# A hybrid streaming encoder on one core: modulation vectors of the reading in and of the first output projection computed on TensorE

## What is computed

```python
cond = silu(c)
for layer in range(4):
    mod = cond @ ada_w[layer] + ada_b[layer]        # 1024 -> 3 * 1024
    shift, scale, gate = split(mod, 3)
    h = rms_norm(x, norm_w[layer]) * (1.0 + scale) + shift
    y = mixer[layer](h)     # RG-LRU, gated DeltaNet, pooling, windowed attention; each ends with @ w_out
    x = x + gate * y
return rms_norm(x, final_norm_w)
```

## Time and profile before

| | |
|---|---|
| median of 3 runs | 3574.63 us (3570.79 to 3578.21) |
| the profiled execution | 3582.37 us |
| its span | 3580.6 us |
| mean granted TensorE clock | 0.968 |
| PE / DVE / ACT / POOL busy, share of the span | 93% / 64% / 42% / 26% |
| instructions | 49279 |

### The profile page before, as it was taken

One profiled execution on the slowest core, in us unless ns is written; L12 is line 12 of the kernel. 1 busy time (PEld: TensorE's weight loads), 2 busy tenths in 40 slices (PEclk: granted clock), 3 DMA queues, 4 the chain that ended last, 5 costly groups with the idle time before them and its releaser, 6 DMA issues.

```text
span 3580.6 us, 49279 instructions
## 1 busy us (share of the span) xinstructions
PE 3331.5 (93%) x18911; PEld 2689.9 (75%) x18911; DVE 2303.9 (64%) x3820; ACT 1509.9 (42%) x2635; POOL 943.0 (26%) x487
## 2 busy tenths in 40 slices
PE   5998899799999999999989999988998999999998
PEld 3776678677887777888767777876778777788877
DVE  6887888763466774565557766996536554556554
ACT  4665365333344124322466655653334431342234
POOL 1003233211233124222510043432121422422233
PEclk9999899899999999999989999998999999999999
DMA  4434455434753532111231123554449221221112
GB/s 170 131 111 129 126 145 147 124 105 127 251 179 89 166 93 88 50 37 36 65 129 55 46 72 84 159 139 111 126 112 349 74 59 53 60 72 40 32 48 100
DMA packets 569015, 383.83 MB, mean 107 GB/s; under 512 B 67802, under 2 KB 522445, under 8 KB 568781
## 3 DMA queue, kind: packets, MB, share of 16 engines
q1 hardware_dynamic: 568781, 380.68, 35.6%
HBM read 299.01 MB, written 80.54 MB: 106 GB/s over the span
## 4 chain that ended last, share of the span: by engine, by line
PE 71%; DVE 16%; DMA 4%; ACT 4%; issue 4%; SPq 1%; POOL 1%; ACTq 0%; DVEq 0%; POOLq 0%
PE bank L230 55%; DVE dnp_conv L1837 3%; DVE dnp_diag_term L1915 2%; DVE h_lo L700 1%; PE bank L2359 1%; DVE res_ada_sums L279 1%; DVE dnp_diag_inv L1918 1%; PE bank L2562 1%; DVE res_h L688 1%; DMA dn_planes<-dnp_inv_t 1%; PE bank L2589 1%; POOL w_lo L212 1%; PE bank L1527 1%; DVE res_sq_total L727 1%; PE bank L2603 1%
## 5 line engine op out<-in xcount | busy, mean ns | idle before, releaser
L230 PE MATMUL bank<-h_hi,w_hi 128*128 128x512 f32 x3616 | 1478.9, 409 | 49.6 <-DVE h_lo L126 16.0
L230 PE MATMUL bank<-h_hi,w_lo 128*128 128x512 f32 x3616 | 1428.0, 395 | 0.0
L230 PE MATMUL bank<-h_lo,w_hi 128*128 128x512 f32 x3616 | 1427.6, 395 | 0.0
L212 POOL TENSOR_TENSOR w_lo<-w_raw,w_hi 128x1024 fp32r<-128x1024 f32 x262 | 648.2, 2475 | 1447.8 <-ACT w_hi L203 1447.8
L230 PEld LDWEIGHTS bank<-h_hi,w_hi 128*128 128x128 f32 x3616 | 691.1, 191 | 227.4 <-issue 57.1
L230 PEld LDWEIGHTS bank<-h_lo,w_hi 128*128 128x128 f32 x3616 | 692.0, 191 | 148.6 <-issue 12.8
L230 PEld LDWEIGHTS bank<-h_hi,w_lo 128*128 128x128 f32 x3616 | 689.7, 191 | 150.8
L1837 DVE SCALAR_TENSOR_TENSOR dnp_conv<-dnp_raw,dn_conv_w,dnp_conv 128x512 f32<-128x512 f32 x288 | 267.1, 928 | 238.4 <-ACT dnp_conv L1659 231.1
L203 ACT ACTIVATE w_hi<-w_raw 128x1024 fp32r<-128x1024 f32 x292 | 306.1, 1048 | 71.5 <-DMA w_raw<-in_pool_w_in 24.8
L757 DVE SCALAR_TENSOR_TENSOR x_res<-bank,mod_gate,x_res 128x512 f32<-128x512 f32 x128 | 95.8, 749 | 268.6 <-PE bank L230 267.8
L844 ACT ACTIVATE res_sq<-x_res 128x512 f32<-128x512 f32 x160 | 101.0, 631 | 327.4 <-DVE x_res L757 225.4
(11 more groups left out here) (321 smaller groups left out, 4485.5 us busy)
## 6 DMA issues: line engine op xcount, KB each, us to landing
dnr_in<-dn_planes SPq DMA_DIRECT2D x112, 512.0 KB, 7.3
dn_planes<-y SPq DMA_DIRECT2D x192, 256.0 KB, 2.5
w_raw<-in_dn_w_in SPq DMA_DIRECT2D x64, 512.0 KB, 4.5
w_raw<-in_swa_w_in SPq DMA_DIRECT2D x36, 512.0 KB, 3.6
w_raw<-in_rg_w_in SPq DMA_DIRECT2D x32, 512.0 KB, 4.8
w_raw<-in_rg_w_out SPq DMA_DIRECT2D x32, 512.0 KB, 3.9
w_raw<-in_dn_w_out SPq DMA_DIRECT2D x32, 512.0 KB, 3.9
w_raw<-in_pool_w_in SPq DMA_DIRECT2D x32, 512.0 KB, 4.4
```

The source lines that it names most:

```text
L212: alu.tensor_tensor(self.lo[j % SLOTS][:, :, :], self.raw[j % 2][:, :, :], self.hi[j % SLOTS][:, :, :].bitcast(F32), ALU.subtract).then_in ...
L230: ins = self.nc.tensor.matmul(out, w[slot][:, k, :], x[:, k, cols], start=(k == 0 and n == 0), stop=(k == KT - 1 and n == 2))
```

## The change

Modulation gets a second way to its result, `multiply`. PE takes each piece as the stationary operand, 128 columns at a time, with column k of cond as the moving operand, and accumulates over k in PSUM bank 3. No running sums are kept (accs is 0), and `accumulate` and `reduce` aren't called in these two phases. PE's products release the pieces' buffers (`used`), and `finish` waits for the last of them. In the reading in PE does piece j after the transposes of step j; in the phase after layer 0 it does four pieces at the end of each of steps 3 to 14. The other two uses of the class stay as they are.

```diff
--- before.py
+++ after.py
@@ -250,6 +250,7 @@
         self.piece = places or [core.sb(f"{tag}_ada{i}", [P, cols], F32, ctx)[:, :] for i in range(bufs)]
         self.bufs = len(self.piece)
         self.acc = [core.sb(f"{tag}_ada_sums{i}", [P, cols], F32, ctx) for i in range(accs)]
+        self.products = 0
         self.loaded = [core.sem(f"{tag}_ada_loaded{i}") for i in range(self.bufs)]
         self.used = core.sem(f"{tag}_ada_used")
         self.summed = core.sem(f"{tag}_ada_summed")
@@ -288,8 +289,24 @@
                                         self.core.ones[:, 0:1], start=True, stop=True)
         ins.then_inc(self.summed, 1)
 
+    def multiply(self, pe, first, last):
+
+        n = self.cols // P
+        for m in range(first, min(last, self.pieces)):
+            t, k = divmod(m, KT)
+            pe.wait_ge(self.loaded[m % self.bufs], 16 * (m // self.bufs) + 16)
+            for i in range(n):
+                ins = self.nc.tensor.matmul(self.bank[:, t * n + i:t * n + i + 1],
+                                            self.piece[m % self.bufs][:, i * P:i * P + P], self.core.cond[:, k:k + 1],
+                                            start=(m == 0 and i == 0), stop=(m == self.pieces - 1 and i == n - 1))
+            ins.then_inc(self.used, 1)
+            self.products = m + 1
+
     def finish(self, dve):
-        dve.wait_ge(self.summed, len(self.blocks))
+        if self.products:
+            dve.wait_ge(self.used, self.pieces)
+        else:
+            dve.wait_ge(self.summed, len(self.blocks))
         core, V = self.core, self.nc.vector
         st = Steps(dve, self.ready)
         for i, (layer, part) in enumerate(self.jobs):
@@ -561,9 +578,9 @@
         ada, late = None, None
         if half == 0 and ingest:
             places = [core.before_h[:, i, :] for i in range(2 * KT)]
-            ada = Modulation(core, ctx, A, [(0, SHIFT), (0, SCALE)], tag, core.bank[3], D, 0, 2, places)
+            ada = Modulation(core, ctx, A, [(0, SHIFT), (0, SCALE)], tag, core.bank[3], D, 0, 0, places)
         elif half == 0 and layer == 0 and depth > 2:
-            late = Modulation(core, ctx, A, [(1, GATE), (2, SHIFT), (2, SCALE)], tag, core.bank[3], CH, 6, 2)
+            late = Modulation(core, ctx, A, [(1, GATE), (2, SHIFT), (2, SCALE)], tag, core.bank[3], CH, 6, 0)
         cs = [slice(c * CH, c * CH + CH) for c in range(NCH)]
         steps = [(c, d) for c in range(NCH) for d in range(KT)]
         split_ab = layer == 0 and depth > 1
@@ -660,8 +677,10 @@
                     sum_squares(c - 1)
                 if final and j > TURN_LAG - 1:
                     turn_x(j - TURN_LAG)
-                if late and j >= 6 and j % 2 == 0:
-                    late.reduce(pe, (j - 6) // 2)
+                if ada:
+                    ada.multiply(pe, j, j + 1)
+                if late and 3 <= j <= 14:
+                    late.multiply(pe, 4 * (j - 3), 4 * (j - 2))
             if final:
                 for j in range(len(steps) - TURN_LAG, len(steps)):
                     turn_x(j)
@@ -669,11 +688,6 @@
                 sum_squares(NCH - 1)
             else:
                 core.sum_last = lambda: sum_squares(NCH - 1)
-            if late:
-                late.reduce(pe, 5)
-            if ada:
-                for t in range(len(ada.blocks)):
-                    ada.reduce(pe, t)
             pe.wait_ge(s_x, len(steps) - 1)
             core.leave(pe, "pe")
 
@@ -768,12 +782,7 @@
                     continue
                 if c > 0 and not ada:
                     norm_dve(dve, c - 1, d)
-                if ada and c > 0:
-                    ada.accumulate(dve, d, d + 1)
-                if late and 3 <= j <= 14:
-                    late.accumulate(dve, 4 * (j - 3), 4 * (j - 2))
             if ada:
-                ada.accumulate(dve, KT, ada.pieces)
                 ada.finish(dve)
                 for k in range(KT):
                     norm_dve(dve, 0, k)
```

## The result

The change makes the kernel slower: 3648.2 us in the median of four runs (3635.4 to 3653.5), against 3574.6 before, a ratio of 1.0192 with a 95% interval of 1.0175 to 1.0209. A second series of the same kernel gave 3649.6 us and 1.0205 (1.0189 to 1.0221). The forecast was 3643, in a range of 3608 to 3668.

A forecast was written before the change was run, and what follows sets the result against it. VectorE was taken to end both stretches before the change; +34 us in the reading in and +34 in the projection on a profiled 3582.4 us gave 3650, less 7.7 us to the runs' median, 3643; range 3608 to 3668.

The forecast's parts named there:

- What bounds the stretches: Reading in and first projection of half 0: VectorE ends last before the change, though TensorE is busy 93% of the span.
- Price of a pair: One weight load and matmul on TensorE: 0.1125 us in a dense stream, 0.22 us in the reading in.
- Reading in: Start of the kernel: 256 pairs on TensorE's path make it +34 us, bounds +5 and +39.
- Piece 0: Reading in: TensorE's first group waits for the first piece, taken to land at 21.0 us.
- POOL's cover: End of the reading in: POOL's subtractions now run beside VectorE's chain instead of beside an accumulation, +2 us.
- The lower bound of +5: Least cost allowed for the reading in, with all pairs at the dense price.
- Projection: First output projection of half 0: 31.3 us removed, 43.2 added, and 22 of clock, sum +34 us, bounds +12 and +89.
- Clock: Projection: ten of twelve thin groups let TensorE's clock fall, 2.2 us lost each, +22 us, bounds 0 and +77.
- (a): Rival: the clock holds through the projection's groups, between dense matmuls; +46 us, 3621; chance 0.17.
- (b): Rival: the pairs keep the clock up everywhere, also in the reading in; +17 us, 3592; chance 0.07.
- (c): Rival, faster: weight loads slip beneath neighbouring work on TensorE in both stretches, 0.06 us a pair, 3558; chance 0.03.
- (d): Rival: clock falls are longer, or TensorE waits for pieces it now releases itself; up to 3698; chance 0.05.

The follow-up runs named there:

- e_reading: Changed kernel with the projection's accumulations put back on VectorE, so only the reading in is changed; 3609.0 us, ratio 1.0096 to the kernel before.
- e_proj: Changed kernel with the reading in's accumulations put back on VectorE, so only the projection is changed; 3625.5 us, ratio 1.0132 to the kernel before.
- e_spread: Changed kernel with each projection step's four pieces split, one behind each 6 dense matmuls instead of four behind 24; 3629.8 us, ratio 1.0143 to the kernel before.
- e_two: Changed kernel with each projection step's pieces put two behind 12 dense matmuls and two behind 24; one run, 3627.4 us.
- e_warm: Changed kernel with three added idle-work matmuls (six before the first piece) ahead of each piece's group in the reading in; one run, 3647.1 us.
- same_before: The kernel before, unchanged, run again for a second profile and its spread; 3575.9 us, ratio 1.0003.
- h_late: Kernel before with the projection's pieces shared, two of each four accumulated on VectorE and two multiplied on TensorE; 3578.9 us, ratio 0.9996 to the kernel before.
- h_both: As h_late, and TensorE also takes four of the reading in's 16 pieces, VectorE the other twelve; 3577.8 us, ratio 0.9996 to the kernel before.
- e_three: Changed kernel with each projection step's pieces put one behind 12 dense matmuls and three behind 24; one run, 3650.8 us.

## Why the prediction was right

It was right in direction and place, and for its own reasons; 3643 us was forecast and 3648 measured. That the sum comes so near is partly luck: the reading in was taken 6 us too high, the projection 3 to 7 too low, and 3 to 7 us more lie behind the first convolution, where the forecast had nothing. By its steps:

- **What bounds the stretches.** DVE ended both before, PE ends both after; in the projection DVE now has 54 us of 173.5. Shown by the profiles of the changed kernel and by e_reading and e_proj. DVE was expected to have 62 us there, as in half 1; why it has less was not looked into.
- **Price of a pair.** 256 and 384 records of L299 were forecast and are there. In the projection the high price of 0.1125 was taken; the groups cost 0.109 where the clock stayed up to their end, and 0.101 in e_spread with the breaks put on the dense matmuls. In the reading in 0.22 was taken and 0.204 measured (3.27 / 16), since groups of one step meet the next transposes without the tail that 3.57 us includes.
- **Reading in.** +34 forecast, +28.3 measured. Piece 0 at 21.0: 21.11. The terms sized too high are the groups, 16 x 3.5 = 56 against 16 x 3.27 = 52, and the transposes, 15 x 1.10 against 15 x 0.89: 1.10 was ScalarE's pace in the kernel before, not PE's cost. The sum of squares was 1.7 and not 2.1. POOL's cover: +2 forecast, +2.9 measured. The first L230 was expected near 100 us and came at 94.9. (The lower bound of +5 leaves out the +2 that the sum has.)
- **Projection.** +34 forecast, +37.5 measured against the first profile of before, +40.8 against the second. The work alone was taken at 104.6 + 43.2 = 147.8 us. An estimate of it from the trace is 173.5 - 58.0 / 2 = 144.5 us, since PE is busy nearly throughout and takes twice as long at the low level; the twelve groups took 3.49 us each where the clock stayed up, 41.9 us and not 43.2. The same estimate gives 148.0 us for e_spread, whose 36 more breaks of 0.1 us are in it. The 31.3 us that the modulation cost before are 27.5 in the second profile of the kernel before (132.5 against 105.0 in half 1), and they held low clock too, 27.3 us of it in each profile. The prediction took them for the load of DVE and PE alone, which made no difference to its sum, as half 1 was its base.
- **Clock.** Ten falls of twelve at 2.2 us, +22, were forecast. There were twelve, and half of their 58.0 us is 29 us, 2.4 each: right in kind, a quarter too low in size. The 173.5 - 151.5 = 22.0 us of e_spread agree with the forecast's number only because e_spread keeps one fall (3.4 us by the same estimate) and has 36 more breaks (3.6 us). This was the term without a row for it, between 0 and 77; its two nearest rows (a fall after 2.40 us of idleness, a fall in thin matmuls) held. Its third return from the low level lasted 6.5 us by the rows, not some 6.
- **Rivals.** (a), the clock holds, falls with the twelve slow starts; its time, 3621, is about that of e_spread and e_two, where it does hold (3630, 3627). (b) falls with 0.204 a pair in the reading in. e_warm shows what it lacked: the pairs and transposes of the changed kernel never raised the clock in 67 us, three dense matmuls a step held it up, and then the pairs are at 0.107. The prediction's evidence that the reading in stays low was one execution, and in four others of the same reading in the transposes did raise the clock for a while (last section); it was right that the changed kernel stays low, on thinner grounds than it had thought. (c) falls: no pair cost less than 0.10. (d): no wait for pieces; its longer falls are there in part, the 29 us for 22.

Open are the 3 to 7 us behind the first convolution, as said above.

## What to carry to other kernels

A matrix-vector product with the matrix stationary pays a full weight load for one column, twice in f32: here 0.21 us for every two loads in the best case, 0.9 us a piece of 128x512, more than the 0.75 that VectorE takes for the same piece. It is worth moving only while TensorE would idle anyway, and TensorE's idle time has to be counted with the clock that it would have there. Where thin work must go between dense matmuls, cut it into short groups: here the same work in groups of 0.8 or 1.7 us cost 22 us less than in groups of 3.5.

## What the runs showed of the hardware

The record of the clock begins, in all twelve profiles, with a rise, and until then the column reads 1.00 whatever the level. It reads 1.00 in the reading in of the changed kernel, where pairs took 0.204 us and four transposes 1.09 us, which are the 1.2 GHz durations (0.107 and 0.63 in e_warm). Before the first recorded change the column doesn't tell the level, the durations do.

Transposes can raise the clock here. The reading in of same_before:

```profile
15.53 5.97 PE L652 MATMUL bank<-ident,y 128*128 128x128 f32 x24 [6.30 <-DMA y<-in_x]
21.99 0.66 PE L652 MATMUL bank<-ident,y 128*128 128x128 f32 x4 [0.48 <-ACT x_res L840]
```

The record has a rise at 20.9 us, and four transposes take 0.66 us from then on; from 21 to 40 us the granted clock is 0.82. e_proj, h_late and h_both, with the same transposes in a row, have such a rise at 17.8 to 20.1 us; the first profile of the kernel before has none, and its transposes stay slow. The six profiles in which all the pairs stand between the transposes and nothing else is added (the changed kernel twice, e_reading, e_spread, e_two, e_three) have none before the first projection.

All twelve groups of 24 pairs in e_three were followed by the low level and, of the 24 groups of 16 in e_two, only the one with a wait in it. I had not expected them to part so cleanly. And a dense stream of matmuls loses 0.1 to 0.14 us at each break for a thin group, beyond the group itself.
